# Hybrid attention, DeltaNet and MoE block: offsets of the first gather, fill transposes, and where a weight load is issued

## What is computed

```
h = h + concat(attn_out, dn_out) @ w_out
logits = rms_norm(h) @ router_w + router_b
top_val, top_idx = top_k(logits, 4); gates = softmax(top_val)
# the 2048 (token, expert) pairs are sorted by expert, each expert padded to whole blocks
for each block of rows of one expert e:
    gu = x_rows @ w_gu[e] + b_gu[e]                     # 1024 x 2048
    act = (clip(up) + 1) * gate * sigmoid(1.702 * gate)
    y[token] += gate_weight * (act @ w_down[e] + b_down[e])   # 1024 x 1024
```

## Time and profile before

| | us |
|---|---|
| median of 3 runs | 1371.28 |
| lowest and highest | 1369.92, 1372.37 |
| the profiled execution | 1371.59 |
| its span in the trace | 1369.8 |
| PE busy | 1210.8 (88%) |
| DVE busy | 504.8 (37%) |
| POOL busy | 283.8 (21%) |
| ACT busy | 206.3 (15%) |
| bytes moved | 446.55 MB, mean 326 GB/s |

### The profile page before, as it was taken

How to read it: one execution, slowest core, us unless ns; L and a number is a source line. 1 busy time by engine, 2 the same in 40 slices (tenths; PEclk the granted TensorE clock), 3 DMA queues, 4 the chain that set the end, 5 groups by cost and what they waited for, 6 DMA issues and landing times.

```text
span 1369.8 us, 30476 instructions
## 1 busy us (share of the span) xinstructions
PE 1210.8 (88%) x12030; PEld 566.0 (41%) x12031; DVE 504.8 (37%) x1213; ACT 206.3 (15%) x415; POOL 283.8 (21%) x381
## 2 busy tenths in 40 slices
PE   7989997989889887979798899988989777799896
PEld 6865554766533332324233333333333222233333
DVE  1236857455333332323233233323333223233332
ACT  4135662133000000000000000000000000000000
POOL 1000004000122222223122223222222222222222
PEclk9999999899799999989899999999999988999999
DMA  6221140439789999999999999999999999998991
GB/s 204 64 67 62 31 123 8 152 147 397 312 346 415 418 419 415 417 419 416 416 417 419 399 381 395 406 403 417 417 421 418 416 421 419 421 415 353 421 408 27
DMA packets 67696, 446.55 MB, mean 326 GB/s; under 512 B 17008, under 2 KB 37688, under 8 KB 43088
## 3 DMA queue, kind: packets, MB, share of 16 engines
q1 hardware_dynamic: 48736, 424.97, 75.1%
q0 software_dynamic: 16176, 18.91, 6.1%
q10 hardware_dynamic: 2752, 2.23, 0.5%
HBM read 435.37 MB, written 15.07 MB: 329 GB/s over the span
## 4 chain that ended last, share of the span: by engine, by line
DMA 46%; PE 37%; DVE 7%; issue 5%; ACT 1%; POOL 1%; SPq 1%; DVEq 1%; POOLq 1%; ACTq 0%
DMA XG<-hn_scratch,IDXC 22%; DMA BDN<-in_expert_b_down 21%; PE PS L636 17%; PE PS L1001 12%; PE PS L1014 4%; DMA out<-Y,IDXS 3%; PE PSC L636 2%; DVE XT L1377 2%; POOL IDXC L391 1%; DVE GU L1386 1%; DMA W<-in_w_in 1%; SPq L208 1%; DVEq L1423 0%; DVE W L1230 0%; DVE W L1231 0%
## 5 line engine op out<-in xcount | busy, mean ns | idle before, releaser
L1001 PE MATMUL PS<-W,XT 128*32 128x512 f32 x5184 | 608.6, 623 | 116.4 <-DVE XT L1377 107.1
L1001 PEld LDWEIGHTS PS<-W,XT 128*32 128x32 f32 x5184 | 169.3, 114 | 516.5 <-issue 409.0
L1014 PE MATMUL PS<-W,AT 128*32 128x256 f32 x5184 | 294.6, 379 | 1.2 <-DVE AT L1397 1.2
L636 PE MATMUL PS<-W 128*128 128x512 f32 (+7 forms) x898 | 250.2, 439 | 10.4 <-DVE W L1175 7.5
L1014 PEld LDWEIGHTS PS<-W,AT 128*32 128x32 f32 x5184 | 169.5, 110 | 145.8 <-issue 47.8
L636 PEld LDWEIGHTS PS<-W 128*128 128x128 f32 (+1 forms) x898 | 151.8, 195 | 95.0 <-issue 75.3
L1386 DVE TENSOR_TENSOR GU<-PS,BGU 128x512 f32<-128x512 f32 x81 | 56.0, 692 | 363.1 <-PE PS L1001 360.4
L409 POOL DMA_INDIRECT out<-Y,IDXS x81 | 130.4, 1610 | 103.5 <-ACT Y L625 96.7
L625 ACT ACTIVATE Y<-SIG,ident 128x256 f32<-128x256 f32 x81 | 41.2, 508 | 656.1 <-DMA out<-Y,IDXS 629.5
L394 POOL DMA_INDIRECT XG<-hn_scratch,IDXC x82 | 87.3, 1064 | 73.4 <-POOL IDXC L391 69.3
L405 POOL COPY IDXS<-IDX 128x1 uint32 (+1 forms) x81 | 14.8, 183 | 391.9 <-DMA out<-Y,IDXS 391.8
(11 more groups left out here) (254 smaller groups left out, 539.9 us busy)
## 6 DMA issues: line engine op xcount, KB each, us to landing
W<-in_expert_w_gate_up SPq DMA_DIRECT2D x128, 2048.0 KB
W<-in_expert_w_down SPq DMA_DIRECT2D x64, 2048.0 KB
W<-in_w_in SPq DMA_DIRECT2D x10, 1024.0 KB, 5.3
W<-in_x SPq DMA_DIRECT2D x8, 512.0 KB, 10.2
W<-in_w_out SPq DMA_DIRECT2D x2, 1024.0 KB, 9.7
W<-in_w_out SPq DMA_DIRECT2D x1, 2048.0 KB, 8.2
hn_scratch<-W POOLq DMA_DIRECT2D x4, 512.0 KB, 11.1
out<-W ACTq DMA_DIRECT2D x4, 512.0 KB, 11.0
```

Of the source, the lines that this page charges most:

```text
L636: return pe.matmul(o, l, r, start=st, stop=sp_)
L1001: last = pe.matmul(GPS[32 * j:32 * j + 32, :].rearrange("p (g n) -> p g n", g=2), XT[:, 32 * k:32 * k + 32], rhs, start=(k == 0), stop=(k ...
L1014: last = pe.matmul(DPS[32 * j:32 * j + 32, :], AT[:, 32 * k:32 * k + 32], DNW[p][:, k, j * QW:(j + 1) * QW], start=(k == 0), stop=(k == KD ...
```

## The change

Four edits, on three engines.

- POOL: the first gather takes its offsets from column 0 of `IDX`. The copy to `IDXC` goes (and the counts of `idx_cur` by one). The waits for `p_a` and `hn_out` stand before the one for `lists_done`. The value load of `LASTB` stands behind the first gather.
- SP: `biases(1, 1)` comes directly after the last gate-up quarter of expert 1. The second half of expert 0's down weights waits for `lists_done` 1 alone.
- SP: the wait for `gathered` goes; the second half of expert 1's down weights waits for `lists_done` 2.
- PE: 2 fill transposes in place of 14 between the matmuls of the gate table and its transpose.

```diff
--- before.py
+++ after.py
@@ -294,10 +294,10 @@
             sp.wait_ge(S_("hn_out"), 16 * NT)
             sp.wait_ge(S_("lg_ps"), NT)
             gu_part(1, 1, [1])
+            biases(1, 1)
+            sp.wait_ge(S_("lists_done"), 1)
+            dn_part(0, 0, [1])
             sp.wait_ge(S_("lists_done"), 2)
-            sp.wait_ge(S_("gathered"), 16)
-            dn_part(0, 0, [1])
-            biases(1, 1)
             dn_part(1, 1, [1])
             def reload(e, p):
                 through = sp.value_load(LASTB[0:1, bass.ds(e - 2, 1)], min_val=0, max_val=MAXB - 1) + 1
@@ -383,13 +383,18 @@
             g.wait_ge(S_("mask"), 3)
             g.wait_ge(S_("msum"), 1)
             g.tensor_tensor(MSUM[:, 1, :], MSUM[:, 0, :], MASK[:, 2, :], ALU.add).then_inc(S_("msum"), 1)
+            g.wait_ge(S_("p_a"), 4)
+            g.wait_ge(S_("hn_out"), 16 * NT)
             g.wait_ge(S_("lists_done"), 1)
-            g.wait_ge(S_("hn_out"), 16 * NT)
-            ahead = g.value_load(LASTB[0:1, NE:NE + 1], min_val=NE - 3, max_val=MAXB - 3)
+            def first_gather():
+                g.sem_inc(S_("passed"), 1)
+                g.indirect_dma_start(out=XG[:, :], out_offset=None, in_=hn_d,
+                                     in_offset=bass.IndirectOffsetOnAxis(ap=IDX[:, 0:1], axis=0),
+                                     bounds_check=ROWS - 1, oob_is_err=False).then_inc(S_("gathered"), 16)
             def gather(i):
                 at = within(i, MAXB, "no routing gives more than MAXB blocks, and one is gathered behind them")
                 g.tensor_copy(IDXC[:, 0:1], IDX[:, bass.ds(at, 1)]).then_inc(S_("idx_cur"), 1)
-                g.wait_ge(S_("idx_cur"), i + 1)
+                g.wait_ge(S_("idx_cur"), i)
                 g.sem_inc(S_("passed"), 1)
                 g.indirect_dma_start(out=XG[:, :], out_offset=None, in_=hn_d,
                                      in_offset=bass.IndirectOffsetOnAxis(ap=IDXC[:, 0:1], axis=0),
@@ -409,8 +414,8 @@
                 g.indirect_dma_start(out=acc_d, out_offset=bass.IndirectOffsetOnAxis(ap=IDXS[:, :], axis=0),
                                      in_=Y[:, :], in_offset=None, compute_op=ALU.add,
                                      bounds_check=ROWS - 1, oob_is_err=False).then_inc(S_("scattered"), 16)
-            g.wait_ge(S_("p_a"), 4)
-            gather(0)
+            first_gather()
+            ahead = g.value_load(LASTB[0:1, NE:NE + 1], min_val=NE - 3, max_val=MAXB - 3)
             next_gather(1)
             next_gather(2)
             g.wait_ge(S_("h_out"), 16 * NT)
@@ -986,7 +991,7 @@
                 t, k = i // TOPK, i % TOPK
                 last = mm(PS[5][0:MAXB + 1, 0:BT], B1[:, t, k, :], TG[:, t, k, :], i == 0, i == 4 * TOPK - 1)
             last.then_inc(S_("gate_ps"), 1)
-            fill(14)
+            fill(2)
             pe.wait_ge(S_("rows4"), 2)
             pe.transpose(GATEP, G4, ident[0:MAXB + 1, 0:MAXB + 1]).then_inc(S_("gl_ps"), 1)
             def gate_up(i, p, rnd, first_of_expert, first):
```

## The result

The changed kernel takes 1375.34 us (median of 17 runs, 1372.42 to 1377.17) against 1371.06 us (17 runs, 1369.18 to 1372.43): a ratio of 1.0032, 95% interval 1.0024 to 1.0040. It is slower by 4.3 us. The number lies in the predicted range (1369.8 to 1376.2), and just inside the forecast's own (1372.6 to 1375.4). It is 1.4 us above the point of 1373.9; as a difference it is 4.3 us where I had 2.6. It lies beyond 0.2%, the side to which I gave 0.34.

A forecast was written before the change was run, and what follows sets the result against it. The dense stream of expert weights bounds the kernel, its refills paced by the first gate-up product's end. A start 1.19 us later plus 1.42 us of slower clock made 2.61 us, so 1373.9 us; range 1369.8 to 1376.2, forecast's own 1372.6 to 1375.4.

The forecast's parts named there:

- the side to which I gave 0.34: Whole kernel: slower by more than 0.2% (2.7 us), chance 0.34, against same 0.56 and faster 0.10.
- POOL's edit: First gather on POOL: without copy and value load ahead, it starts at 352.65 instead of 353.79, descriptors out 1.14 us sooner.
- The lead of the instruction: POOL, before the first gather's instruction: 0.97 us from the copy's end, of which 0.9 was kept.
- The load on the gather: First gather beside 2 MB of early down weights: 6.0 us from descriptors to rows, so rows at DVE 2.14 us later.
- Rival 1: First gather slips in where the old weights end, at 355.0; kernel 1371.8 to 1372.4 us; chance 0.19.
- The 0.68 us from turn to product: From the start of DVE's turn of the rows to the first gate-up product where PE is free: 0.68 us.
- The fills and the clock: First gate-up product on PE: with 12 fills fewer PE idles 3.5 us, and half clock lengthens the product by 1.42 us.
- The row that I had taken: The third gate-up product before the change: 9.48 us long after 4.09 us of idling, the model for the clock's price.
- My sign for this: A first product of 8 us in the changed profile would show that the fills weren't what held the clock.
- The transposes and the clock: PE before the change: sixteen fills alone raised the grant from 0.50 to 1.00, against the skill's rule that transposes do not.
- the sum of 1.19 us: First product's later start, and the whole delay instead of 2.61 us if dropping fills costs no clock.
- First product's end: First gate-up product on PE: ends 1.19 + 1.42 = 2.61 us later, at 369.9 for 367.3.

The follow-up runs named there:

- a2: The kernel before with SP's edits alone, all 14 fills kept: 1375.24 us against 1371.57, ratio 1.0026.
- a3: The changed kernel with 14 fills instead of 2: 1374.36 us, ratio 1.0020 to the kernel before.
- a4: The changed kernel with both halves of the first down weights (4 MB) issued at the index table's end: 1375.39 us against 1371.57, ratio 1.0026.
- b1: The changed kernel with 12 transposes added at PE's very start, where PE idles: 1374.22 us against 1370.13 for the kernel before, ratio 1.0032.
- c1: The kernel before, unchanged, run and traced a second time: ratio 0.9994.
- c2: The kernel before, its 14 fills kept, with 12 more transposes at PE's very start, so longer code: ratio 0.9993.
- b4: The kernel before with PE's edit alone, 2 fills instead of 14: 1372.63 us against 1370.13, ratio 1.0017.
- a1: The changed kernel with SP as before, so only POOL's and PE's edits: 1372.49 us against 1371.57, ratio 1.0006.
- c3: The changed kernel, 12 transposes at PE's start, early half of the first down weights held until the first gather landed: 1371.86 us against 1370.93, ratio 1.0009.
- b2: POOL's and PE's edits with SP as before, plus 12 transposes at PE's very start: 1371.64 us against 1370.13, ratio 1.0008.

## Why the prediction came out as it did

**POOL's edit: right in kind, its gain too large.** I took 1.14 us off the descriptors; after has them at T + 2.52 for T + 3.19, 0.67 less. From T to the gather's instruction were 1.43 us, not 0.95: in the row of after this idle is put down to issue. The lead of the instruction, taken from a gather behind a copy, did not hold for one behind a semaphore of another engine; what fills the 1.43 us no row shows.

**The load on the gather: right.** I took 6.0 us from descriptors to rows; after has 6.09, a2, a3, a4 and b1 5.76, 6.09, 6.20 and 6.17, and with dry queues it is 2.05 to 2.72 (before, c1, c2, b4, a1, c3). Rows were 2.70 us later than before for 2.14 predicted, and 0.47 of the difference is POOL's error.

**Rival 1 fell, and with it the reading of a packet as a transfer's share.** The gather's descriptors were out at 355.85, and its first packets moved at 359, 3.15 us later. The old weights had ended well before: in b2, whose descriptors were out at the same moment after T, the old weights ended 0.95 us behind them, and with no new ones there the gather moved at once. a4, with a further transfer behind, is like after. The Trainium skill, DMA: Bandwidth & Descriptors, "Queues, rings and completion order", lets an engine change queues at the end of a packet. If a transfer's share were one packet, the gather would have had its turn when the old weights' share ended, and the rival's gain with it; its packets moved only after that. The rule with a smaller packet is not touched by this. What the runs show is a wait of about 3.2 us to the first packet behind weights, the same with 2 or 4 MB queued and with runs of 4 or 16 KB.

**The 0.68 us from turn to product: right** (0.69 in after).

**The fills and the clock: near in size, the cause not the one I gave.** I added 1.42 us for the missing fills; after's product is 1.04 longer than before's. The fills aren't what made the difference. Where the rows were prompt, the grant rose between T + 9.2 and T + 9.6 in six traces, with 14 fills (before, c2) and with 2 (b4, a1, b2, c3); in the seventh, c1, it rose before the product began, though its code is that of before. In b4, with T at 352.51, it rose 9.2 us after T:

```profile
361.50:362.00 0.50, 0.50 (x12) 0.08 (x8) 0.00 (x0) 0.00 (x0) 0.00 (x0) 0.80 1.01 426
```

So the products with 2 fills (8.97, 9.00, 8.50 and 8.40 us against 8.06 and 8.04) are longer because they start sooner, with more of them ahead of the rise, and they end sooner too (T + 14.3 to 15.2 against T + 15.6). With late rows the grant rose at T + 12.5 to 13.4, at T + 13.0 with 14 fills (a2, a3) and on either side of that with 2. So the longer product came with the late rows, fills or not. The row that I had taken, a product after 4.09 us of idling, resembles after's in its idle of 4.08 us, but the length of the idle doesn't settle it: b2 idled 1.58 us and the grant rose at T + 9.5, a3 1.69 us and it rose at T + 13.0. Why late rows put the rise off stays open. My sign for this, a first product of 8 us if the fills weren't what held the clock, could not tell the two apart.

**The transposes and the clock.** c1 supports the row of transposes that the prediction set against the Trainium skill, TensorE: Matmul & The Clock Gate, "Part 4: PE-mode transpose": its grant rose within 359.5 to 360 (0.81), while PE ran its 14 fills. But the sum of 1.19 us that I had put beside that rule misses for another reason: the clock's price came with the late rows, with or without fills.

**First product's end: 2.80 us later for 2.61 predicted.** Against the trace that I predicted from, the sum to this point stands. That it comes this close is partly that trace: against c1 the end is 4.25 us late, against c2 2.82.

**What the sum lacked: that all that follows shifts by this much.** I had looked only for what would absorb the shift. The idle before the third product, a row that I used for the clock, I took as fixed. It rose from 4.09 to 5.64 us. In the five kernels with 2 fills and shorter code it is 0.6 to 1.6 us above that of before, in the three with 2 fills and the old length of code (b1, b2, c3) -0.2 to 0.4, so it is a term of PE's edit, by the length of code, that my sum lacks. With it the third product is 4.35 us late. At the end of the span 2.57 of this are left in the two traces compared (1020.67 less 1018.10), 4.2 against c1, and by medians 4.3. Two traces of the kernel before differ by 1.6 in the rest and 1.4 in T, so single traces do not settle the last microsecond. How much of the idle's 1.6 us reaches the end is not settled either. Over the thirteen traces the rest of the span grows by some 0.8 us for each us that the third product starts later, an estimate by a straight line through the table; yet b1, which takes the longer idle away, is no faster by medians, though its interval is 1.6 us wide either way.

The mechanism that I had put first, the load on the gather, was right and makes most of the loss. My point was 1373.9, the measured time 1375.34. With a point of 2.6 us I had called a difference within 0.2% (2.7 us) the likeliest; the 1.7 us that the loss was larger put it beyond.

## What to carry over

A load that nobody waits for isn't free if it fills a queue that stood dry while a small, awaited transfer was on its way: here 2 MB issued 8 us early cost the first gather 3 to 4 us and the kernel about 0.25%. Before moving such a load, look at the DMA share in the microseconds in which each awaited transfer flies. And where a chain of products sets when refills are issued, delay at its head shifts the whole stream, so count every microsecond up to there, the idle put down to issue too. And take a second trace of the kernel before: here it moved the apparent lag of the first product by 1.4 us.

## What I had not expected of the hardware

The rows of a gather issued from POOL beside weights in runs of 16 KB are there 5.8 to 6.2 us after its descriptors are out, against 2.1 to 2.7 with dry queues, and the same for 2 and 4 MB queued. Its first packets wait some 3.2 us, behind runs of 4 KB as well. The first product in PE's loop over experts starts 3.7 to 4.0 us after a packet of 16 KB on the queue of instructions, and 12 transposes placed elsewhere in the program shift the idle before it by 0.8 to 1.7 us (before and c2, a1 and b2, after and b1). And the moment T moved by 2.4 us between traces of kernels that have the same code up to it, which at 0.2% of the time is as much as some of the effects studied here.
